# Routing inside the out projection: ranks for pairs of tiles, the choice behind the norm row, and the order of the first loads of the experts

## What is computed

```python
x = x + jnp.concatenate([y_s5, y_dn], axis=-1) @ w_out[i]
h = _rmsnorm(x, norm_ffn[i]).reshape(bsz * seq, d)
# _hier_moe
_, g_sel = lax.top_k(h @ w_rg + b_rg, 1)            # 1 of 4 groups
top_val, top_idx = lax.top_k(e_logits, TOP_K)       # 2 of its 8 experts
order = jnp.argsort(flat_e)                         # assignments sorted by expert,
...                                                 # in blocks of 128 slots
hid = jax.nn.silu(xb @ w_gate[e]) * (xb @ w_up[e])
return hid @ w_down[e]
```

## Time and profile before

| what | us |
|---|---|
| median of 3 runs | 1447.84 |
| lowest, highest | 1447.61, 1449.54 |
| profiled execution, its own time | 1460.46 |
| its span from first to last instruction | 1458.8 |
| TensorE busy | 1323.0 (91%) |
| DVE busy | 1099.8 (75%) |
| ACT busy | 862.4 (59%) |
| POOL busy | 413.7 (28%) |

### The profile page before, as it was taken

One profiled execution on the slowest core, in us unless ns is written; L12 is line 12 of the kernel. 1 busy time (PEld: TensorE's weight loads), 2 busy tenths in 40 slices (PEclk: granted clock), 3 DMA queues, 4 the chain that ended last, 5 costly groups with the idle time before them and its releaser, 6 DMA issues. The chain is left out here.

```text
span 1458.8 us, 24962 instructions
## 1 busy us (share of the span) xinstructions
PE 1323.0 (91%) x8416; PEld 1113.2 (76%) x8416; DVE 1099.8 (75%) x1502; ACT 862.4 (59%) x1162; POOL 413.7 (28%) x479
## 2 busy tenths in 40 slices
PE   4999899977888979899974899999999999999984
PEld 3999788867888878668863688888888888888851
DVE  6895797766677658635656888888888888888827
ACT  7473344564555554641213588878878887788722
POOL 5020099027656737221101111111111111111140
PEclk9999999988898989999985899999999999999997
DMA  9174988212233139700016899999999999999773
GB/s 264 59 229 123 304 244 228 76 40 55 53 104 101 26 147 344 267 29 29 30 44 235 307 394 416 412 414 410 409 407 414 407 410 410 409 415 415 310 273 138
DMA packets 154969, 357.51 MB, mean 245 GB/s; under 512 B 44015, under 2 KB 100619, under 8 KB 127499
## 3 DMA queue, kind: packets, MB, share of 16 engines
q1 hardware_dynamic: 132043, 297.04, 54.7%
q0 software_dynamic: 14976, 40.43, 8.1%
q10 hardware_dynamic: 7872, 19.01, 3.3%
HBM read 287.64 MB, written 68.78 MB: 244 GB/s over the span
## 5 line engine op out<-in xcount | busy, mean ns | idle before, releaser
L2868 PE MATMUL gate_up_mm<-w_hi,gathered_T_hi 128*128 128x512 f32 x528 | 213.3, 404 | 10.8 <-DVE gathered_T_lo L3058 10.8
L2870 PE MATMUL gate_up_mm<-w_hi,gathered_T_lo 128*128 128x512 f32 x528 | 208.5, 395 | 0.0
L2869 PE MATMUL gate_up_mm<-w_lo,gathered_T_hi 128*128 128x512 f32 x528 | 207.8, 393 | 0.0
L3053 DVE TENSOR_TENSOR w_lo<-w_down,w_hi 128x2048 fp32r<-128x2048 f32 x66 | 148.6, 2289 | 53.4 <-ACT w_hi L2976 53.3
L3053 DVE TENSOR_TENSOR w_lo<-w_gate,w_hi 128x2048 fp32r<-128x2048 f32 x66 | 150.9, 2290 | 13.8 <-ACT w_hi L2976 12.9
L2800 POOL COPY gather_idx<-upto_pair 128x1 int32 (+1 forms) x34 | 9.4, 278 | 522.5 <-PE x_turned L2858 476.0
L2976 ACT ACTIVATE w_hi<-w_up 128x2048 fp32r<-128x2048 f32 x66 | 126.6, 1920 | 52.1 <-PE down_mm L2905 49.9
L3053 DVE TENSOR_TENSOR w_lo<-w_up,w_hi 128x2048 fp32r<-128x2048 f32 x66 | 150.8, 2288 | 4.3 <-ACT w_hi L2976 0.2
L2976 ACT ACTIVATE w_hi<-w_gate 128x2048 fp32r<-128x2048 f32 x66 | 126.7, 1919 | 38.4 <-PE gate_up_mm L2870 32.0
L2976 ACT ACTIVATE w_hi<-w_down 128x2048 fp32r<-128x2048 f32 x66 | 125.1, 1918 | 39.7 <-issue 18.2
L2868 PEld LDWEIGHTS gate_up_mm<-w_hi,gathered_T_hi 128*128 128x128 f32 x528 | 100.8, 191 | 37.1 <-issue 12.0
(11 more groups left out here) (523 smaller groups left out, 3106.9 us busy)
## 6 DMA issues: line engine op xcount, KB each, us to landing
w_gate<-in_expert_w_gate SPq DMA_DIRECT2D x66, 1024.0 KB, 8.0
w_up<-in_expert_w_up SPq DMA_DIRECT2D x66, 1024.0 KB, 8.1
w_down<-in_expert_w_down SPq DMA_DIRECT2D x66, 1024.0 KB
expert_rows_dram<-ones SPq DMA_DIRECT2D x32, 512.0 KB, 6.6
expert_rows_dram<-expert_out ACTq DMA_DIRECT2D x32, 512.0 KB, 8.6
x<-s_rows_dram SPq DMA_DIRECT2D x9, 1184.0 KB, 7.5
s_rows<-s_rows_dram SPq DMA_DIRECT2D x7, 1184.0 KB, 6.7
w_raw<-in_w_in SPq DMA_DIRECT2D x12, 512.0 KB, 5.2
```

The costliest lines, as they stand in the source:

```text
L2868: pe.matmul(dst, xT_hi[:, k, :], hi[:, at, cols], start=k == 0, stop=False)
L2869: pe.matmul(dst, xT_hi[:, k, :], lo[:, at, cols], start=False, stop=False)
L2870: mm = pe.matmul(dst, xT_lo[:, k, :], hi[:, at, cols], start=False, stop=k == KT - 1)
L3053: dve.tensor_tensor(lo[:, at, :], flat(j), hi[:, at, :].bitcast(F32), ALU.subtract).then_inc(S["piece_lo"], 1)
```

## The change

In the projection:

- `pick(t-1)` moves ahead of the add into x on DVE, so that mean, reciprocal and norm row follow the add directly. `logit(t-1)` comes after 10 pieces of the tile instead of 12. `hT` has one buffer instead of two.
- Ranks are made for pairs of tiles (0,1), (2,3), (4,5) in tiles 3, 5 and 7, with 64 columns at a time, and for 6 and 7 singly in the tail. DVE keeps running sums for every tile, copies the ranks out of PSUM (`read`) and places two tiles one behind the other. Tables come in pairs in tiles 5 and 7. The count of all tiles is one matmul at the end instead of two.
- The norm's weights are loaded earlier, and the whole gate weight of expert 0 (2 MB) is loaded once the mixers' sums are no longer needed.

At the head of the experts:

- SP waits for the first gather to land before it issues the up weights. ACT turns the rows of block 0 before it splits the up weights, and DVE takes the pieces in the same order.
- POOL's six instructions for constants go; index row and bounds are kept from the routing, and DVE makes the rest itself.

```diff
@@ tensor
-                pe.wait_ge(Q["summed"], t + 1)
+                if t in READ_BEFORE:
+                    pe.wait_ge(Q["read"], READ_BEFORE[t])
...
-            def rank(t):
-                pe.wait_ge(Q["both"], t + 1)
-                pe.wait_ge(Q["summed"], t + 1)
-                pe.matmul(pos_ps, r["strict"][:], r["both"][:, t % 2], start=True, stop=False)
-                mm = pe.matmul(pos_ps, c["ones"][:], r["sum"][:], start=False, stop=True)
...
+            def rank(n):
+                tiles = RANKED[n]
+                dst, first, end = pos_ps[:, 0:NEXP * len(tiles)], tiles[0], tiles[-1] + 1
+                pe.wait_ge(Q["both"], end)
+                pe.matmul(dst, r["strict"][:], r["both"][:, first:end].rearrange("p t e -> p (t e)"), start=True, stop=False)
+                pe.matmul(dst, c["ones"][:], r["sum"][:, first:end].rearrange("p t e -> p (t e)"), start=False, stop=True
+                          ).then_inc(Q["ranked"], 1)
...
                 project(t, 0, 8)
-                if t >= 2:
-                    rank(t - 2)
-                if t >= 3:
-                    table(t - 3)
+                if t in (3, 5, 7):
+                    rank((t - 3) // 2)
+                if t in (5, 7):
+                    for n in RANKED[(t - 5) // 2]:
+                        table(n)
                 if t >= 1:
                     route(t - 1)
-                project(t, 8, 12)
+                project(t, 8, 10)
                 if t >= 1:
                     logit(t - 1)
-                project(t, 12, 16)
+                project(t, 10, 16)
@@ vector
+            def read(n):
+                dve.wait_ge(Q["ranked"], n + 1)
+                width = NEXP * len(RANKED[n])
+                dve.tensor_copy(r["pos"][:, 0:width], pos_ps[:, 0:width]).then_inc(Q["read"], 1)
+                dve.wait_ge(Q["read"], n + 1)
...
-                places(TTo(r["prod"][:], one, twice(pos_ps), ALU.mult))
+                places(TTo(r["prod"][:], one, twice(pos), ALU.mult))
...
             for t in range(TT):
-                if t >= 2:
-                    place(t - 2)
+                if t == 1:
+                    dve.wait_ge(Q["made"], ROUTE_MADE)
+                if t in (3, 5, 7):
+                    read((t - 3) // 2)
+                    for n in RANKED[(t - 3) // 2]:
+                        place(n)
+                if t >= 1:
+                    pick(t - 1)
                 dve.wait_ge(Q["mm"], t + 1)
                 dve.tensor_tensor(x1[:, t, :], x1[:, t, :], mm_ps[:, t % 2].rearrange("p a n -> p (a n)"), ALU.add
                                   ).then_inc(Q["x1"], 1)
-                if t == 1:
-                    dve.wait_ge(Q["made"], ROUTE_MADE)
-                if t >= 1:
-                    pick(t - 1)
@@ sync
+            sp.wait_ge(S["out"], 8)
+            sp.dma_start(nf[:], a["norm_ffn"].partition_broadcast(P)).then_inc(Q["par"], 16)
             sp.wait_ge(S["gated_turned"], TT)
-            sp.dma_start(nf, a["norm_ffn"].partition_broadcast(P)).then_inc(Q["par"], 16)
+            sp.dma_start(w_first[:], a["expert_w_gate"][0, 0].rearrange("(p k) n -> p k n", k=KT)
+                         ).then_inc(Q["first"], 16)
...
-            for j in range(4):
+            for j in range(2):
+                sp.sem_inc(ld[j], 16)
+            sp.wait_ge(gathered[0], 16)
+            for j in (2, 3):
                 load(j, 0)
@@ scalar
-            for j in range(4):
+            for j in range(2):
                 split(0, j, 16, None)
             rows_out(0)
+            for j in (2, 3):
+                split(0, j, 16, None)
+RANKED = ((0, 1), (2, 3), (4, 5), (6,), (7,))
+READ_BEFORE = {2: 1, 4: 2, 6: 3, 7: 4}
```

## The result

The changed kernel takes 1430.47 us (median of 4 runs, 1427.47 to 1433.42), the kernel before 1448.69 (4 runs): ratio 0.9871, interval 0.9844 to 0.9899, so 14.6 to 22.6 us less. The direction and the places were right; the sum was some 3 us too small. Two repetitions further on, each on another chip, gave 0.9888 and 0.9884 (16.2 and 16.8 us).

The account below looks back on a forecast made before the run. TensorE was taken to bound the expert loop, untouched by the change, so only the loop's start could move. Gains of 7.3 + 2.4 + 3.9 = 13.6 us took the median 1447.84 to 1434.2, range 1431 to 1440.

Parts of the forecast that it names:

- the tail: After the projection's last tile: the last norm row comes 2.4 us earlier, and with smaller gains and losses 2.4 is gained.
- the head: Start of the experts up to block 1: gain 3.9 us, bounds 5.6 and -0.4 depending on the gather's landing.
- Tiles: Projection tiles: TensorE's waits for the norm row go, 10.2 us freed, some given back for ranks and tables, 7.3 left.
- the 0.4 I had added: Tiles 3 and 5: DVE's first placement held 0.4 us by POOL's second subtraction, so both placements end at 11.5.
- My sign for the odd tiles: Projection, odd tiles: 14.4 to 15.1 us between adds into x would show the forecast right.
- My split into 1.7 for the weights and 2.0 for the waits: Head of the experts: of the 3.9 us gain, 1.7 from the weights, 2.0 from the waits, the rest rounding.
- The 13.5 for block 0: Experts' block 0 on TensorE: its 48 matmuls, the first dozen at the lower clock, take 13.5 us, ending at 804.9.
- The up weights come late: Rival, experts' head: ordering the up weights behind the gather costs more than it gives; 1438.5 us at 9.4; chance 0.14.
- The rule on descriptors: Experts' head: GpSimd's descriptors wait for DVE holding the shared pair; first gather 2.46 us on POOL, 1.4 later, 1435.6.
- Doubled placements: Rival, tiles 3 and 5: both placements meet POOL at full price, 6.4 us more, 1440.6; chance 0.13.
- Cheaper than thought: Rival: gather off the path and rank pairs as cheap as single ones, 1431.5 us; chance 0.08.
- Clock: Rival, projection: TensorE granted 1.2 GHz, each matmul up to 0.236 us longer, all 336 giving 1500; slower, chance 0.03.

Follow-up runs that it names:

- again: The kernel before, unchanged, run once more against the kernel before on the same chip: ratio 1.0012 (0.9995 to 1.0030).
- order_alone: Changed kernel with the pairs undone (single ranks, placements and tables per tile), the choice still ahead of the add: 1428.84 us, ratio to before 0.9900.
- routing_only: Changed kernel's projection with the experts' head of the kernel before: 1439.20 us, ratio to before 0.9929.
- up_at_once: Changed kernel, but the experts' first up loads are issued at once and do not wait for the first gather: 1434.94 us, ratio to before 0.9898.
- changed_again: The changed kernel, unchanged, run once more on another chip: 1427.21 us against 1443.66 for the kernel before, ratio 0.9888.

## Why the prediction was right and wrong

**The mechanism was right; the step that failed is the size of two terms, the tail (2.4, measured 3.4) and the head (3.9, measured 5.0).** Predicted 7.3 + 2.4 + 3.9 = 13.6. Measured by stage, before against after 7.8 + 3.4 + 5.0 = 16.3 (added before rounding), again against the two repetitions 7.7 + 3.8 + 5.4 = 16.9, and by the ratios of the repetitions 16.2 and 16.8. Applied to the 1447.84 from which I started that is 1430.9 to 1431.6, the lower edge of my range. The first comparison's median was another 1 to 2 us better; with four runs and an interval of 8 us that is variation, and no experiment shows a further gain.

**Tiles: 7.3 predicted, 7.8.** By stage my figure is 7.0, because the add of tile 7, which I had 0.3 late and charged to the tail, ends the seven tiles. The step by step held. In tile 3, counted from the add at 662.11: rank read at 6.0 (I had 6.15 to 6.4), both placements done at 11.4 (11.5), the choice at 15.6 (15.7), TensorE late by 0.27 afterwards (0.2). The first product was held once in each of tiles 3 and 5, 0.60 and 0.61 against 0.22, until POOL's subtraction ended: the 0.4 I had added. The Trainium skill, "SBUF — State Buffer", section "Who interferes with whom", has such pairs of operations take one port pair in turn; the trace agrees, with 0.4 and not the 1.3 of the worst case. The missing half microsecond is in the ranks and tables: a rank of 64 columns took 0.39 of TensorE's time (667.87 - 667.48; one of 32 in order_alone 0.36) and a rank with two tables 0.92 (696.88 - 695.96), where I had 0.5 and 1.1. My sign for the odd tiles, 14.4 to 15.1 between adds, missed (15.59, 15.59 and 15.21), and it did not follow from my own working, which has the choice end at 15.7 and the add behind it. What I did not see is that the logits' move, which I put at nothing, carries 3.2 of the term, and that the pairs, which give the change its name, carry 0.6. The 1.0 for the norm's weights came as forecast (1.1).

**Tail: 2.4 predicted, 2.7 without tile 7's late add, 3.4 to 3.9 measured.** Two terms were too small. The logits started 2.9 earlier after the add (6.73 against 9.63), not 2.4: the transposes came 2.5 earlier, and the table of tile 5 no longer stands between them and the logits. And from the choice to the product it was 1.65 instead of 2.20, 0.55 where I had 0.8 - 0.5 = 0.3. In the repetitions the last eight transposes took 1.24 and 1.13 instead of 1.60, which is most of their further 0.4.

**Head: 3.9 predicted, 5.0 to 5.4.** The term that was mis-sized is the arrival of the second up load. I had the up loads start 6.3 after the experts' begin and land 8.0 later; they started 5.7 after it (gather landed in 4.6, not 5.1) and the second was there 7.4 after its issue. Together 1.1 to 1.2, and that is the whole difference to 5.0: DVE's last up remainder ended 17.4 after the start instead of 18.5, and block 1 came at 33.0 instead of 34.1. The further 0.4 in the repetitions is 0.25 from the old head (38.25 in again) and the rest from the new one; against routing_only's 36.93 the gain would be 4.1, close to my 3.9 only by luck, since I reckoned from 38.0. My split into 1.7 for the weights and 2.0 for the waits was not what the experiments found: 2.7 for the weights with the order of the up loads (0.8 of it the order), 1.6 for the constants. The 13.5 for block 0 does not come out of its own terms either (36 x 0.236 + 12 x 0.472 = 14.2; from its first gate matmul to the transposes of block 1 it took 781.46 - 767.33 = 14.1), but nothing hung on it.

**The rivals.** The up weights come late: fell, since the gather took 4.6 to land, and up_at_once shows that the order gives 0.8. The rule on descriptors ("SBUF: two separate sides" of the same page of the Trainium skill) would, as I used it, have made POOL's first gather 2.46. It took 1.09, so it did not bear here: DVE ran only short operations beside it. In the loop the gather starts inside one of DVE's remainders and ends 0.85 after it (in after 805.49 + 2.45 = 807.94, where the remainder of 804.80 ends at 807.09; in sixteen such gathers of before, after and changed_again 0.84 to 0.86). The gather of block 2 (787.69) starts between remainders and takes 0.98, which fits a wait for that remainder; no run moved the two apart. Doubled placements: fell, the longest hold was 0.4 and no wait in the tiles was over 0.27. Cheaper than thought (1431.5, 0.08): nearest to the truth in time and right about the rank pairs; the gather stayed on the path, since the up loads wait for it. Clock: fell, 1.00 in the projection; all 336 matmuls at the lower level would have been 336 x 0.236 = 79 more, so 1513 and not 1500.

## What to carry to other kernels

- When one engine's long serial chain feeds the next tile, order inside the tile comes before batching: the choice ahead of the add and the logits two pieces sooner gave 6 us, and pairing added 0.6 on top of it; with the pairs but not the order the tiles were 1.2 longer than before. Price every small move by what waits for it, not by its own length.
- Behind a removed wait ask which operation on the same chain is wanted only much later: sixteen operations moved behind block 1 gave 3.5 us, and the same ones on an engine that takes 1.54 us for each instead of 0.26 gave it back at the end of the loop.
- In a program whose executions vary by 0.3%, sums of a few us must be read by stage, against repetitions of both kernels; medians of five and six runs did not show 3.2 us that the sum of seven tiles showed.

## What was not expected of the hardware

- TensorE after its pause ahead of block 0 was back at a granted 1.00 after 3.5 us in one kernel and 6 in another, with the same instructions in block 0: the head differed by 1.3 us (36.93 and 38.25). What sets it was not tried.
- A gather's instruction on POOL takes 1.0 to 1.1 us between DVE's remainders, and 2.2 to 2.5 in the loop, where it starts beside a remainder of DVE (w_lo, two inputs in SBUF) and ends 0.85 after it.
- The last stage, same code, took 54.3 to 54.9 us on one chip and 46.5 to 47.8 on two others. DVE's second addition of rows gathered from DRAM came 17.9 after the last norm's load in up_at_once and 10.7 in changed_again, which is the whole difference of these two last stages; why those rows came later was not tried.
- A 128x128 one-hot operation took 0.26 on DVE and 24.62 / 16 = 1.54 on POOL, beside DVE's remainders.
